# A three-part edit to a hybrid attention / mixture-of-experts backbone on one core: the barrier of the expert stages, one activation-table load, and the transposes of the first norm

## What is computed

```python
for l in range(2):
    mod, mod_c = silu(c) @ ada_w[l] + ada_b[l], silu(c_ctx) @ ada_w[l] + ada_b[l]   # six vectors of 1024 each
    h, hc = modulate(rms_norm(x, norm_mix[l]), sh_m, sc_m), modulate(rms_norm(xc, norm_mix[l]), sh_mc, sc_mc)
    o_c, o = na_gqa_mixer(hc, h, ...) if l == 0 else diff_mixer(hc, h, ...)          # attention, both streams
    x, xc = x + g_m * o, xc + g_mc * o_c
    tokens = modulated rms_norm of x (and of xc in layer 0)
    x, xc += g_f * moe_ffn(tokens, ...)     # 64 experts, top 8 per token, and a shared expert
return rms_norm(x, final_norm)
```

## Time and profile before

| | us |
|---|---|
| median of 3 runs | 1861.3 (1860.07 to 1863.41) |
| the profiled execution, its own time | 1861.2 |
| its span, first to last instruction | 1859.4 |
| PE busy | 1654.0 (89% of the span) |
| DVE busy | 564.2 (30%) |
| ACT busy | 316.1 (17%) |
| POOL busy | 208.5 (11%) |

### The profile page before, as it was taken

One profiled execution on the slowest core, in us unless ns is written; L12 is line 12 of the kernel. 1 busy time (PEld: TensorE's weight loads), 2 busy tenths in 40 slices (PEclk: granted clock), 3 DMA queues, 4 the chain that ended last, 5 costly groups with the idle time before them and its releaser, 6 DMA issues. The chain is left out here.

```text
span 1859.4 us, 23133 instructions
## 1 busy us (share of the span) xinstructions
PE 1654.0 (89%) x8531; PEld 738.8 (40%) x8531; DVE 564.2 (30%) x1329; ACT 316.1 (17%) x690; POOL 208.5 (11%) x197
## 2 busy tenths in 40 slices
PE   4999998999999999999997499888789999979896
PEld 2644444454334343334333244455333333333332
DVE  2041676365222222222121552274421111111112
ACT  1101443130111111111111111172100010100002
POOL 0300343001111111111110000040000000000000
PEclk7999999999999999999999699999899999999998
DMA  9422994026999999999995943202799999999993
GB/s 352 130 91 98 380 367 143 7 101 258 418 396 407 421 416 404 403 412 402 415 414 244 378 164 115 70 1 80 317 419 401 419 414 410 417 419 413 418 406 125
DMA packets 125649, 560.81 MB, mean 302 GB/s; under 512 B 17570, under 2 KB 22961, under 8 KB 75360
## 3 DMA queue, kind: packets, MB, share of 16 engines
q1 hardware_dynamic: 107104, 512.22, 68.8%
q0 software_dynamic: 17248, 43.62, 6.2%
q10 hardware_dynamic: 1184, 3.47, 0.5%
HBM read 549.95 MB, written 26.80 MB: 310 GB/s over the span
## 5 line engine op out<-in xcount | busy, mean ns | idle before, releaser
L1705 PE MATMUL ps<-wb,pool 128*32 128x512 f32 (+2 forms) x2608 | 487.4, 599 | 17.4 <-issue 17.4
L1705 PEld LDWEIGHTS ps<-wb,pool 128*32 128x32 f32 (+2 forms) x2608 | 159.3, 124 | 306.2 <-issue 306.0
L1719 DVE TENSOR_TENSOR ffn_hid<-ffn_sg,ps 128x256 f32<-128x256 f32 x71 | 29.9, 421 | 606.2 <-ACT ffn_sg L1713 606.2
L1749 PE MATMUL ps<-pool,ffn_hidT 128*32 128x512 f32 (+2 forms) x584 | 164.7, 598 | 21.9 <-DVE ffn_hidT L1734 11.4
L1749 PE MATMUL ps<-hT,ffn_hidT 128*32 128x512 f32 (+2 forms) x680 | 156.5, 597 | 19.6 <-DVE ffn_hidT L1734 14.7
L1612 POOL DMA_INDIRECT pool<-h_rows,ffn_index x71 | 75.6, 1065 | 630.6 <-PE ps L1675 306.6
L2351 PE MATMUL ps<-wb,hT 128*128 128x512 f32 x320 | 140.2, 600 | 1.6 <-issue 1.6
L1713 ACT ACTIVATE ffn_sg<-ps 128x256 f32<-128x256 f32 x71 | 27.2, 383 | 487.3 <-PE ps L1705 487.3
L1749 PE MATMUL ps<-sh_wd,ffn_hidT 128*32 128x512 f32 (+2 forms) x272 | 100.3, 597 | 4.7 <-DVE ffn_hidT L1734 2.7
L1767 PE MATMUL ps<-x_res,rw 128*128 128x512 f32 x224 | 103.1, 603 | 0.9 <-ACT x_res L1795 0.9
L1675 PEld LDWEIGHTS ps<-const,pool 128*128 128x128 f32 x568 | 77.4, 194 | 65.2 <-issue 61.8
(11 more groups left out here) (315 smaller groups left out, 1765.6 us busy)
## 6 DMA issues: line engine op xcount, KB each, us to landing
wb<-in_expert_w_gate_dram SPq DMA_DIRECT2D x108, 1024.0 KB, 13.7
wb<-in_expert_w_up_dram SPq DMA_DIRECT2D x108, 1024.0 KB, 17.1
pool<-in_expert_w_down_dram SPq DMA_DIRECT2D x52, 1024.0 KB, 18.6
hT<-in_expert_w_down_dram SPq DMA_DIRECT2D x52, 1024.0 KB, 18.8
wb<-in_ada_w_dram SPq DMA_DIRECT2D x24, 2048.0 KB, 11.5
sh_wd<-in_expert_w_down_dram SPq DMA_DIRECT2D x24, 1024.0 KB, 19.0
mix_yr<-y_rows SPq DMA_DIRECT2D x7, 2048.0 KB, 11.7
wb<-in_diff_w_in_dram SPq DMA_DIRECT2D x6, 2048.0 KB, 16.4
```

The source lines that it names most:

```text
L1705: mm = nc.tensor.matmul(core.ps[lo:lo + width, gu_bank(n), :], xT[:, n % 2, k, lo:lo + width], w[:, k], start=k == 0, stop=k == KD - 1, sk ...
L1719: nc.vector.tensor_tensor(hid[:, n % 2, :], sg[:, n % 2, :], core.ps[:, gu_bank(n), F:2 * F], ALU.mult).then_inc(hid_ready, 1)
L1749: mm = nc.tensor.matmul(core.ps[lo:lo + width, down_bank(half), :], hidT[:, n % 2, k, lo:lo + width], wd_at(q % DR, half, k), start=k == 0 ...
```

## The change

1. The block of `feed_forward` (both layers) is opened with `no_gpsimd_drain=True`. In the built program the end of these blocks no longer holds a Drain on GpSimd; the four reports and the release stay. On the other engines the Drain and the report become two instructions.
2. The one-element Sqrt of layer 1 stands behind the overflow branch.
3. `norm_transpose` is gone as a stage. The constants are loaded in two parts (`ident` and `pick`, 130 columns, ahead of the first `ada_w` block; the other 1125 columns ahead of the projection weights). The transposes of the context rows stand between the second block's sums and its columns, and are copied raw into `hT`; those of the latent rows stand around the fourth block's columns. When the modulation is known, the context part of `hT` is modulated in place and the latent part out of its banks. The banks of the sums go from four to two, those of the columns from two to one.

```diff
-for _name, _n in (("ident", P), ("flip", P), ("before", P), ("ones", P), ("iota", 512), ("pick", 2), ("fours", P // 4),
+for _name, _n in (("ident", P), ("pick", 2), ("flip", P), ("before", P), ("ones", P), ("iota", 512), ("fours", P // 4),
...
+        items = [(s, k) for s in range(STREAMS) for k in range(KD)]
+        on_act = lambda n: n in (2, 5, 7) or n >= KD and n % 4 >= 2
...
-        m = Modulation(core, st, [(0, b) for b in range(MOD_FIRST)], 0, [0, 1, 2, 3], [4, 5])
+        m = Modulation(core, st, [(0, b) for b in range(MOD_FIRST)], 0, [0, 1], [4])
...
+                sp.dma_start(core.const[:, 0:early], a["consts"][:, 0:early]).then_inc(const_in, 16)
                 core.stream.feed(sp, 2, 0)
-                sp.dma_start(core.const[:], a["consts"][:, 0:CONST_W]).then_inc(const_in, 16)
...
+                sp.dma_start(core.const[:, early:], a["consts"][:, early:CONST_W]).then_inc(late_in, 16)
                 core.stream.feed(sp, MOD_FIRST + STREAM, 0, m.used)
+                sp.wait_ge(late_in, 16)
...
+                    if i == 1:
+                        for n in range(1, KD, 2):
+                            act.wait_ge(turned, n + 1)
+                            nc.scalar.copy(raw(n), turn_at(n)).then_inc(taken[1], 1)
+                act.wait_ge(mod_ready, 1)
...
+                for n in range(len(items)):
+                    if on_act(n):
+                        act.wait_ge(turned, n // 2 * 2 + 2)
+                        out, src, amp, shift = modulated(n)
+                        nc.scalar.activation(out, src, ACT.Identity, scale=amp, bias=shift)
...
                 for n in range(MOD_FIRST):
                     m.pe_sums(pe, n)
...
+                    if n == 1:
+                        pe.wait_ge(norm.row_ready, 2)
+                        turn(0, KD)
+                    if n == 3:
+                        pe.wait_ge(norm.row_ready, TILES)
+                        for e in range(2):
+                            pe.wait_ge(taken[e], KD // 2)
+                        turn(KD, KD + 4)
+                    m.pe_columns(pe, n)
+                    if n == 3:
+                        turn(KD + 4, 2 * KD)
+                    if n == 2:
+                        pe.wait_ge(rows_in, 48)
+                        nc.tensor.transpose(core.ps[:, 5, 0:P], rows[:], core.c("ident")).then_inc(rowsT, 1)
...
-        norm_transpose(core, 0, 0, [0, 1])
...
-        with nc.Block() as block:
+        with nc.Block(no_gpsimd_drain=True) as block:
...
-                else:
-                    nc.scalar.activation(table_of[:], core.c("ident")[:, 0:1], ACT.Sqrt)
                 further(act, over, None, lambda b, e, n: fb_act(act, b, e, n))
                 if last:
+                    nc.scalar.activation(table_of[:], core.c("ident")[:, 0:1], ACT.Sqrt)
```

More of the change, by code:

```diff
@@ L546, in modulation @@
         rows = st.sb("rows", [P, P])
+        hT = core.hT[:].rearrange("p k (s c) -> p k s c", s=STREAMS)
+        early = CONST["pick"][1]
+        items = [(s, k) for s in range(STREAMS) for k in range(KD)]
+        on_act = lambda n: n in (2, 5, 7) or n >= KD and n % 4 >= 2
+        turned, taken = st.sem("turned"), [st.sem("taken_dve"), st.sem("taken_act")]
+        mod_ready, late_in = st.sem("mod_ready"), st.sem("late_in")
         cond = st.sb("cond", [P, STREAMS, KD])
@@ L581, in _, with turn @@
             @block.tensor
             def _(pe):
+                def turn(lo, hi):
+                    for n in range(lo, hi):
+                        s, k = items[n]
+                        if s == 0 and n >= 4:
+                            pe.wait_ge(taken[n % 2], n // 2 - 1)
+                        for j in range(2):
+                            mm = nc.tensor.transpose(turn_at(n)[:, j * P:(j + 1) * P],
+                                                     core.xn[:, 2 * s + j, k * P:(k + 1) * P], core.c("ident"))
+                        mm.then_inc(turned, 1)
@@ L605, in _ @@
                     m.dve_part(dve, n)
[L606 to L612, removed]
-                m.dve_finish(dve, link)
[L616 to L629, removed]
-        with nc.Block() as block:
[L632 to L660, removed]
@@ new lines, in _ @@
+                    if n == 1:
+                        norm.dve_rows(dve, 0)
+                        norm.dve_rows(dve, 1)
+                        for j in range(0, KD, 2):
+                            dve.wait_ge(turned, j + 1)
+                            nc.vector.tensor_copy(raw(j), turn_at(j)).then_inc(taken[0], 1)
+                    m.dve_take(dve, n)
+                    if n == 2:
+                        norm.dve_rows(dve, 2)
+                        norm.dve_rows(dve, 3)
+                        dve.wait_ge(rowsT, 1)
+                        link(nc.vector.tensor_copy(core.cols[:], core.ps[:, 5, 0:P]))
@@ L665, in rotate @@
+                m.dve_finish(dve, link)
+                dve.sem_inc(mod_ready, 1)
+                dve.wait_ge(taken[0], KD // 2)
+                dve.wait_ge(taken[1], KD // 2)
+                for n in range(len(items)):
+                    if not on_act(n):
+                        dve.wait_ge(turned, n // 2 * 2 + 2)
+                        out, src, amp, shift = modulated(n)
+                        nc.vector.tensor_scalar(out, src, amp, shift, ALU.mult, ALU.add)
 def rotate(nc, link, pairs, tmp, cos, sin):
```

20 lines of the change are left out of this document (13 added, 7 removed).

## The result

| | before | after |
|---|---|---|
| median | 1861.3 (5 runs, 1860.07 to 1863.41) | 1850.0 (5 runs, 1849.01 to 1853.07) |
| the profiled execution, its own time | 1861.2 | 1849.0 |
| its span | 1859.4 | 1847.2 |
| PE busy | 1654.0 | 1647.1 |

The ratio is 0.9939, with a 95% interval of 0.9927 to 0.9951: 11.3 us faster, where 7.3 was forecast. Five more runs of the same kernel later gave 1853.0 (ratio 0.9952, 0.9938 to 0.9965). One run of e12 took 2036.1 us at a mean granted clock of 0.84 and is left out of the figures of that experiment.

What follows compares the result with a forecast made beforehand. TensorE and DMA were taken as full in most slices, the edits sitting at three serial joints; 6.0 + 0 + 1.0 + 0.3 = 7.3 off 1861.2, plus 0.1 for the median, gave 1854.0 us, range 1850.8 to 1858.4.

Steps and rivals of the forecast that it cites:

- the case for faster: Whole kernel: a time below 1857.6 us, given a chance of 0.82.
- Part 1: Barrier from ffn0 to mix1: without GpSimd's drain mix1's first load goes out 6.0 us earlier; ffn1's drain gives 0.
- Part 2: End of the kernel: the Sqrt table load between square and root goes off the path, 1.0 us gained.
- Part 3: First stage: projection starts 2.4 us earlier, less 2.1 us for a start at half clock, net 0.3 us.
- The rival of a dear issue: First stage: the small constants piece takes 4.36 us to issue instead of 0.45, total 1857.9 us; chance 0.12.
- 16 transposes at 0.20: First stage: the context rows' transposes, 0.20 us each, done at 29.4 us, in a chain reaching the projection at 49.6.
- nothing has raised the clock: Ahead of the projection: TensorE idle from about 46.5 to 49.6 us behind short work, so the projection starts at half clock.
- The cold start: Start of the first projection: matmuls run 4.3 us at half speed, as seen in mix1, losing 2.1 us.
- the first stage pays after all: First stage: the denser TensorE queue raises the clock early and holds it, 3 us instead of 0.3, 1851.3 us; chance 0.13.
- Against: at 28 us the clock is low with TensorE busy all the time: First stage: the forecast's argument against the rival that a denser TensorE queue raises the clock early (chance 0.13).

Runs made afterwards that it cites:

- e12: The changed kernel with 28 identity transposes ahead of the first projection and 32 at the head of mix1, in its second set of runs: 1850.6 us.
- e2: The kernel before with only the barrier changed (no GpSimd drain in the feed_forward blocks): 1854.9 us.
- e4: The kernel before with GpSimd's drain left out at the end of ffn1 only: 1861.7 us.
- e3: The kernel before with only the one-element Sqrt moved behind the overflow branch: 1860.5 us.
- e1: The kernel before with only the new first stage, barrier and Sqrt table as before: 1858.0 us.
- e6: The changed kernel with its 16 context transposes split 8 and 8, the second group behind the third block's sums: 1850.4 us.
- e10: The changed kernel with 32 identity transposes added at the head of mix1: 1851.8 us.
- e5: The kernel before with 16 identity transposes added on TensorE ahead of the fourth block's sums: 1859.5 us.
- e9: The changed kernel run once more, unedited: 1853.0 us.
- e8: The changed kernel with 28 identity transposes added in TensorE's gap ahead of the first projection: 1852.5 us.

## Why the prediction was wrong

The direction, the case for faster and two of the three terms held; the third failed. That the first five runs fell outside the range and the second five inside is scatter: the term is wrong for both.

- **Part 1, 6.0: right.** 6.04 in the changed kernel, 5.65 in e2. The reason held too: the last scatter's landing, at 2.6 us, and nothing else stood behind the drain. The load came 2.65 us after the issue; 2.7 was given. ffn1's drain was worth 0, as e4 shows.
- **Part 2, 1.0: right.** 1.0 by the rows in the changed kernel and in e3. The rule of the Trainium skill ("ScalarE: Activation LUTs", "What ACT_TABLE_LOAD costs": load and drain at each switch) would have given an estimated 2.4, and the root would have moved by that much; it moved by 1.0. The rows decide against the second half of the rule here.
- **Part 3, 0.3: wrong.** It was 5.1 between the profiled executions and 4.0 (2.0 to 5.4) in e1.
- The issue of the small piece was put at 0.45 and took 0.43; the 4.36 of the old piece went to whatever stood behind the two blocks (3.64 for the context rows). The rival of a dear issue falls. The context rows landed at 20.9 (forecast 20.6) and their transposes began at 26.05 (26.2).
- **The step that failed** is the chain behind "16 transposes at 0.20": every piece of it was priced at the lower clock. The one reason, "nothing has raised the clock", stands behind the chain, for the projection's start. In the trace the clock rose at 29.3, while the 16 transposes ran, and two sums, three groups of columns and the latent rows' transposes took 1.92, 0.95 to 1.05, and 0.13 each. So the modulation was known at 40.1 where 45.9 stood.
- The projection therefore started at 44.16, not at 49.6. Even with a later rise (e1, e6, e10) it started at 44.8 to 46.7. In every trace of the new first stage the clock was up for the fourth block's sums (1.92), in none of the four unedited ones of the old stage (3.64).
- How the 7.9 us divide shows with e5 between the two traces: the held clock in the old order gives 4.35 (52.02 to 47.67), the moved work and the earlier landings another 3.5 (to 44.16), where 2.4 was forecast for the moved work. The cold start takes 2.8 back. These are single traces.
- **The cold start, 2.1: right in kind.** Measured 2.8 (5.6 us instead of 4.3 at half speed). The "two per us" and "four per us" of the forecast count matmuls cut by a window's edge; the rates are 1.2 and 2.3, and the factor of two is the same. 0.50 was granted at 44 us, behind 4.2 us of waiting; this agrees with the Trainium skill ("TensorE: Matmul & The Clock Gate", Part 1), by which an idle TensorE starts at half rate.
- The modulation pieces in place were put at 0.25 and took 0.34 (1.70 / 5); 3.8 us for 3.4 to 3.6, a small error the other way.
- The rival *the first stage pays after all* (0.13) named the right mechanism and was mis-sized: it gave 3 where 5.1 came (4.0 in e1). Its price took the gain as an upper bound of +3 (no cold start, transposes partly warm), and never worked out the whole chain at full clock. That sum, 2 x 1.7 for sums, 3 x 0.75 for columns and 16 x 0.07 for transposes, 6.8 us, was to be had from the earlier trace rows by halving what ran at 0.50, and would have put the low end of the range at about 1847.
- "Against: at 28 us the clock is low with TensorE busy all the time" holds in e2 too, but says nothing of the time behind it. In before the clock stayed low to 50 us. In e2, with the same code, it was up from 39.9 to 43.3, which took 1.3 us off the 16 columns (2.29 for 3.57):

```profile
28.00:29.00 1.00, 1.00 (x12) 0.25 (x8) 0.00 (x0) 0.00 (x0) 0.00 (x0) 0.50 1.04 373
...
42.00:43.00 1.00, 0.00 (x0) 0.00 (x0) 0.64 (x4) 0.00 (x0) 0.00 (x0) 1.00 1.06 378
```

Before's profiled execution was one whose first stage stayed low to the end. Measured against the four traces with the old first stage (projection at 49.5 to 52.0), part 3 gains 5.7 at the start on average (five turned traces: 44.16, 44.18, 45.44, 44.83, 46.67, mean 45.1, against 50.8), less 2.8 for the cold start: 2.9, within e1's interval. By the last scatter of ffn0 the same traces are 4.3 apart (1016.1 and 1011.8 on average), near e1's 4.0. So of the 5.1 of the profiled pair some 2 are the luck of the pair.

What stays open: why the rise comes at 29.3 us in two runs (the changed kernel, e9) and at 33.0 to 35.4 in others (e1, e10, e12) of the same code, and so whether it is the 16 transposes (3.5 us in one piece) or TensorE's other work around them that brings it. No run here fixes it. Why e9's set lay 3 us above the first is put down to such stretches by its one profile alone; of its other runs there is no trace.

## What to carry to other kernels

Before pricing a chain of TensorE pieces that a change makes denser, work it out once at each clock level and let the range reach both ends: what runs behind the rise of the clock in a dense queue takes half the time, and a serial stage gets the difference up to the next transfer it has to wait for (here the fourth block, at 34.66). At a barrier, look at what the last engine to arrive waits for and whether the next stage needs it; a drain whose own data have landed is worth the rest of its length, and one in front of longer work of another engine is worth nothing (6.0 and 0 here, of 8.1 and 9.1). And take the baseline's clock from more than one trace where a stage hangs on it.

## What the runs showed of the hardware that was not expected

- GpSimd's drain at the end of a block took 8.1 us although the last scatter landed 2.6 us after its issue, and 9.14 in ffn1; with it gone, the scatter's data were seen at the same 2.65 us. Its length is not the transfer's.
- The issue time on SP goes with the place in the queue: the same transfer of context rows took 1.14 us to issue behind the constants (before) and 3.64 directly behind the two blocks of 2 MB (changed kernel). The constants took 4.36 us in that place; their small piece took 0.43 in front of the blocks, but it is also a tenth of the bytes.
- The moment when the granted clock changes moved by several us between executions of the same instructions (projection at 49.60, 49.52, 51.89 and 52.02 in unchanged code). The total does not follow one for one: e4's projection was 2.5 us earlier than before's, and its profiled execution only 0.4 shorter (1860.8 for 1861.2). Filling TensorE's idle time with work whose result nobody reads gained 2.8 us once (e5), and nothing that could be told in the times in two other places (e8, e10, and both in e12).
